# Seven half-block products for the third feed-forward block of a two-layer recurrent trunk

## What is computed

```python
def swiglu(x, wg, wu, wd):
    return (jax.nn.silu(x @ wg) * (x @ wu)) @ wd
...
        x = x + 0.5 * swiglu(rmsnorm(x, ng[0]), prm['ffn_w_gate'][layer, 0], prm['ffn_w_up'][layer, 0], prm['ffn_w_down'][layer, 0])
        hn = rmsnorm(x, ng[1])
...
        x = x + 0.5 * swiglu(rmsnorm(x, ng[2]), prm['ffn_w_gate'][layer, 1], prm['ffn_w_up'][layer, 1], prm['ffn_w_down'][layer, 1])
```

## Time and profile before

| | |
|---|---|
| median of 3 runs | 2454.22 us (2450.13 to 2454.34) |
| the profiled execution | 2454.07 us, span 2452.2 us |
| TensorE (PE) busy | 2386.2 us, 97% |
| VectorE (DVE) busy | 1455.3 us, 59% |
| ScalarE (ACT) busy | 855.2 us, 35% |
| GpSimd (POOL) busy | 399.8 us, 16% |

### The profile page before, as it was taken

The page is one execution under the profiler, slowest core; times in us unless marked ns, Lnnn a source line. Parts: engine busy times, 40 slices in busy tenths (PEclk is TensorE's granted clock), DMA queues, the critical chain, the costliest instruction groups (busy, mean ns, idle before and its releaser), DMA issues.

```text
span 2452.2 us, 44056 instructions
## 1 busy us (share of the span) xinstructions
PE 2386.2 (97%) x18653; PEld 2266.3 (92%) x18653; DVE 1455.3 (59%) x1953; ACT 855.2 (35%) x1198; POOL 399.8 (16%) x524
## 2 busy tenths in 40 slices
PE   7999999999999999999999999999999899999999
PEld 7999999999799999999999999988555589999998
DVE  7856955677755443334343436832788766666654
ACT  5533534453432222223222223334444332222222
POOL 0201200132001122000000000001221113444432
PEclk9999999999999999999999999999999999999999
DMA  4333334232124555332323332322445546888974
GB/s 130 104 104 88 101 89 140 83 87 72 48 78 147 166 157 111 95 88 86 93 87 94 102 91 78 94 71 58 155 155 155 169 134 222 288 296 292 300 240 166
DMA packets 445201, 325.53 MB, mean 133 GB/s; under 512 B 15321, under 2 KB 392453, under 8 KB 444909
## 3 DMA queue, kind: packets, MB, share of 16 engines
q1 hardware_dynamic: 428120, 274.90, 38.2%
q0 software_dynamic: 13232, 42.10, 4.8%
q10 hardware_dynamic: 3728, 6.87, 0.8%
HBM read 278.95 MB, written 44.99 MB: 132 GB/s over the span
## 4 chain that ended last, share of the span: by engine, by line
PE 85%; DVE 8%; DMA 2%; issue 2%; ACT 2%; SPq 0%; POOL 0%; DVEq 0%; POOLq 0%; ACTq 0%
PE ps L2436 65%; PE ps L2529 8%; PE ps L3012 3%; DMA m_c_ring<-in_state_mlstm_C 2%; PE ps L2798 2%; DVE m_qcs L2200 1%; PE ps L2632 1%; PE ps L2940 1%; DVE m_acc L2200 1%; PE ps L2986 0%; PE ps L2927 0%; DVE m_rstd L1494 0%; PE ps L2691 0%; DVE m_tmp L2212 0%; PE ps L2926 0%
## 5 line engine op out<-in xcount | busy, mean ns | idle before, releaser
L2436 PE MATMUL ps<-m_n_hi,m_w_hi 128*128 128x260 f32 x3136 | 635.6, 284 | 5.3 <-DVE m_w_lo L1479 5.3
L2436 PE MATMUL ps<-m_n_hi,m_w_lo 128*128 128x260 f32 x3136 | 632.4, 283 | 0.0
L2436 PE MATMUL ps<-m_n_lo,m_w_hi 128*128 128x260 f32 x3136 | 631.3, 283 | 0.0
L1479 DVE TENSOR_TENSOR m_w_lo<-m_w_raw,m_w_hi 128x1024 fp32r<-128x1024 f32 (+1 forms) x268 | 355.0, 1324 | 327.4 <-ACT m_w_hi L813 276.2
L2436 PEld LDWEIGHTS ps<-m_n_hi,m_w_hi 128*128 128x128 f32 x3136 | 484.3, 189 | 8.5 <-issue 5.0
L2436 PEld LDWEIGHTS ps<-m_n_hi,m_w_lo 128*128 128x128 f32 x3136 | 484.0, 189 | 0.0
L2436 PEld LDWEIGHTS ps<-m_n_lo,m_w_hi 128*128 128x128 f32 x3136 | 482.9, 188 | 0.0
L813 ACT ACTIVATE m_w_hi<-m_w_raw 128x1024 fp32r<-128x1024 f32 (+1 forms) x252 | 279.7, 1110 | 201.0 <-PE ps L2436 194.9
L2436 PE MATMUL ps<-m_h_hi,m_w_hi 128*128 128x260 f32 x1056 | 212.9, 283 | 0.0
L2436 PE MATMUL ps<-m_h_hi,m_w_lo 128*128 128x260 f32 x1056 | 212.3, 282 | 0.0
L2436 PE MATMUL ps<-m_h_lo,m_w_hi 128*128 128x260 f32 x1056 | 211.9, 282 | 0.0
(11 more groups left out here) (518 smaller groups left out, 4082.8 us busy)
## 6 DMA issues: line engine op xcount, KB each, us to landing
m_w_raw<-in_ffn_w_down SPq DMA_DIRECT2D x64, 704.0 KB, 4.7
m_w_raw<-in_ffn_w_gate SPq DMA_DIRECT2D x68, 512.0 KB, 4.2
m_w_raw<-in_ffn_w_up SPq DMA_DIRECT2D x68, 512.0 KB, 4.0
m_c_ring<-in_state_mlstm_C SPq DMA_DIRECT2D x128, 256.0 KB, 3.6
m_u_ring<-in_state_mlstm_C SPq DMA_DIRECT2D x128, 256.0 KB, 5.9
out_C_s<-m_u_ring POOLq DMA_DIRECT2D x128, 256.0 KB, 5.6
m_w_raw<-in_ev_w_in SPq DMA_DIRECT2D x32, 512.0 KB, 4.1
m_w_raw<-in_ml_w_in SPq DMA_DIRECT2D x32, 512.0 KB, 4.1
```

The source lines that it names most:

```text
L1479: v.tensor_tensor(w_lo[:, j % 2, 0:kt * P], w_raw[:, j % 2, 0:kt * P], w_hi[:, j % 2, 0:kt * P].bitcast(F32), ALU.subtract).then_inc(S("w_ ...
L2436: last = mm(out[:, t, :], w[:, j % 2, c], r[:, k0 + k, t * HT:(t + 1) * HT], start=start and k == 0 and n == 0, stop=stop and k == kt - 1 ...
```

## The change

The third FFN takes the seven-product form too: one plain tile (two units) and then 21 blocks, 10 in the first lot and 11 in the second, each lot followed by its 8 down units. The second FFN stays plain, but is done in two lots as well: 22 units, 8 down units that are added to `x`, 22 units, 8 down units. During the last 8 of them the tokens are put in the layout of the third FFN (`n_high_s`, `token_parts`, `token_sums`, `token_high`, `token_low`). The 28 loads of POOL are issued behind the last block of the third FFN, and the transposes and `gate_weights` that use them move into its last 8 down units. In the first FFN, the operations of ACT and DVE around its three plain tiles stand in another order, and the second lot's down units use two pairs of PSUM banks instead of four. Loops of the second and third FFN are written out. The code's helpers have an index `q` now: 0 for the first FFN, 1 for the third.

```diff
--- before.py
+++ after.py
-NP = 3
+STG = (0, 2)
+NPS = (3, 1)
...
+        late_at = (s_at, cur[0] - 4 * T * 4)
...
-        BLOCKS = [(0, i, f) for i, f in enumerate(range(NP, FB))] + [(1, i, f) for i, f in enumerate(range(FB, KF))]
-        FIRST, LAST = (0, FB - NP), (FB - NP - 1, KF - NP - 1)
+        BLOCKS = [(q, c, i, f) for q in range(2) for c in range(2) for i, f in enumerate(range(c * FB if c else NPS[q], (c + 1) * FB))]
...
-        dn_pair = lambda c, d: ((2 + d) % 4, d % 4)[c]
+        dn_pair = lambda c, d: ((2 + d) % 4, d % 2)[c]
...
+                elif c == 0 and i == 0:
+                    sp.wait_ge(S("w_lo"), PLAIN_END[q])
+                elif c == 0 and i == 1:
+                    sp.wait_ge(S("f_tl"), NT * (q + 1))
...
             for i in range(4):
                 pool.wait_ge(S(f"u_kept{i}"), 64)
+            for b in range(FIRST[1][0], len(BLOCKS)):
+                weight_sums(b)
+            pool.wait_ge(S("f_mm"), product(LAST[1][1], "P4"))
...
+            def first_tiles():
+
+                token_high(0, 0)
                 norm_root(0, by_rstd)
                 first_high(4)
-                token_high(1)
                 first_high(5)
-                token_parts(4)
-                token_parts(5)
-                gate(0, 0)
-                token_parts(6)
-                token_parts(7)
-                token_high(2)
-                h_high(0, 0)
-                gate(1, 1)
-                token_high(3)
-                h_high(1, 1)
+                token_high(0, 1)
+                token_parts(0, 4)
+                token_parts(0, 5)
+                gate(0)
+                token_parts(0, 6)
+                token_parts(0, 7)
+                token_high(0, 2)
+                h_high(0)
+                token_high(0, 3)
+                gate(1)
                 a_high(0)
-                gate(2, 2)
+                b_high(0)
+                h_high(1)
+                gate(2)
...
+            def third_tiles():
+
+                token_high(1, 3)
+                a_high(FIRST[1][0])
+                norm_root(NORM_S[1], by_rstd)
+                b_high(FIRST[1][0])
...
+                        if b not in (FIRST[0][0], FIRST[1][0]):
+                            b_high(b)
...
+            def ffn_plain():
+
+                for c in range(2):
+                    u0 = first_unit["up1"] + c * (2 * FB + KD)
+                    for f in range(FB):
+                        u, n = u0 + 2 * f, KF + c * FB + f
+                        hi(u + 1, 1, KD)
+                        if n == KF:
+                            norm_root(NORM_OF[1], by_rstd)
+                            hi(u + 2, 0, KD)
+                        gate(n)
+                        if n > KF:
+                            hi(u + 2, 0, KD if f + 1 < FB else FB)
+                        h_high(n)
+                    u = u0 + 2 * FB
+                    for d in range(KD):
+                        hi(u + d + 1, d + 1, FB if d + 1 < KD else KD)
                         if c:
-                            if d + 2 < KD:
-                                dn_high(c, d + 2)
-                            elif d + 1 == KD:
-                                hi(first_unit["in_e"], 0, KD)
-                            n_high(X_STAGE["dn0"], d)
-                            square(X_STAGE["dn0"], d, d % 2)
-                        else:
-                            if d + 2 < KD:
-                                dn_high(c, d + 2)
-                            if d == 2:
-                                a_high(FIRST[1])
+                            if d + 1 == KD:
+                                hi(u + KD + 1, 1, KD)
+                            n_high_s(1, d)
+                            square(NORM_S[1], d, d % 2)
+                            token_parts(1, d)
+                            if d in (2, 4, 6):
+                                token_high(1, d // 2 - 1)
...
+            def first_tiles():
+
+                token_sums(0, 0)
+                token_sums(0, 1)
+                token_low(0, 0)
                 first_low(4)
-                norm(0, by_rstd)
-                dve.wait_ge(S("r_ev"), 1)
-                plain(0)
                 first_low(5)
-                token_low(1)
-                token_sums(2)
-                plain_up(0)
-                token_low(2)
-                token_sums(3)
-                plain(1)
-                token_low(3)
-                plain_up(1)
+                rows_factor(0)
+                plain(0, 0)
+                token_low(0, 1)
+                token_sums(0, 2)
+                plain_up(0, 0)
+                token_low(0, 2)
+                token_sums(0, 3)
+                token_low(0, 3)
+                plain(1, 2)
+                lot_low(0, A_LOT)
+                plain_up(1, 2)
                 dve.wait_ge(S("f_tl"), NT)
-                h_low(0, 0)
-                h_low(1, 1)
-                lot_low(0, A_LOT)
-                plain(2)
-                plain_up(2)
+                h_low(0)
+                lot_low(0, B_LOT)
+                h_low(1)
+                weight_sums(0)
+                plain(2, 4)
+                plain_up(2, 4)
+
+            def third_tiles():
+
+                b, u = FIRST[1][0], first_unit["up2"]
+                token_sums(1, 3)
+                token_low(1, 3)
+                lot_low(b, A_LOT)
+                lot_low(b, B_LOT)
+                weight_sums(b)
+                rows_factor(NORM_S[1])
+                plain(F0[1], u)
+                lot_low(b, C_LOT)
+                lot_low(b + 1, A_LOT)
+                plain_up(F0[1], u)
...
+                        if q and c and 4 <= d < 7:
+                            gate_weights(d - 4, 0)
+                            gate_weights(d - 4, 1)
+                        down_out(c, d, u, X_R[q] + KD * c, xs)
...
+                    for f in range(FB):
+                        u, n = u0 + 2 * f, KF + c * FB + f
+                        lo(u + 1, 1, KD)
+                        if n == KF:
+                            lo(u + 2, 0, KD)
+                            rows_factor(NORM_OF[1])
+                        plain(n, u)
+                        new_state(u)
+                        if n > KF:
+                            lo(u + 2, 0, KD if f + 1 < FB else FB)
+                        plain_up(n, u)
+                        h_low(n)
+                    if c:
+                        acc_clear(xs)
+                    for d in range(KD):
+                        u = u0 + 2 * FB + d
+                        lo(u + 1, d + 1, FB if d + 1 < KD else KD)
+                        down_out(c, d, u, 2 * KD + KD * c, xs)
+                        if c:
+                            if d + 1 == KD:
+                                lo(u + 2, 1, KD)
+                            n_low_s(1, d)
+                            acc_add(xs, d, d % 2)
+                            if d in (2, 4, 6):
+                                token_low(1, d // 2 - 1)
+                            if d in (1, 3, 5):
+                                token_sums(1, d // 2)
...
+                        if d >= 4 - 2 * c:
+                            pe.wait_ge(S("x_r"), X_R[q] + KD * c + d - 3 + 2 * c)
...
+                        if q and c and d == 4:
+                            pe.wait_ge(S("ld_conv"), 16)
+                            for k in range(KM):
+                                last = nc.tensor.transpose(ps[:, 5, k * NS * 3:(k + 1) * NS * 3], c_stage[:, k * P:(k + 1) * P], ident[0:NS * 3, 0:NS * 3])
+                            last.then_inc(S("cbuf_tr"), 1)
...
-            up(1, 2)
-            down("dn1", KU, 2, h_hi, h_lo, "h_lo", KF)
-            up(2, 3)
-            pe.wait_ge(S("ld_conv"), 16)
-            pe.wait_ge(S("g_r"), 3 * KF)
-            for k in range(KM):
-                last = nc.tensor.transpose(ps[:, 5, k * NS * 3:(k + 1) * NS * 3], c_stage[:, k * P:(k + 1) * P], ident[0:NS * 3, 0:NS * 3])
-            last.then_inc(S("cbuf_tr"), 1)
-            down("dn2", KU, 2, h_hi, h_lo, "h_lo", 2 * KF)
+            ffn_plain()
+            third_tiles()
+            ffn_s(1)
```

More of the change, by code:

```diff
@@ L571, in _ @@
+            ffn_s(0)
             for u, (g, h) in enumerate(EV):
@@ new lines, in third_tiles @@
+            def third_tiles():
+                u0 = first_unit["up2"]
+                for u in range(2):
+                    pe.wait_ge(S("w_lo"), u0 + u + 1)
+                    for k in range(KD):
+                        if u == 0:
+                            pe.wait_ge(S("xn"), KD * NORM_S[1] + k + 1)
+                        last = plain(u, k)
+                    last.then_inc(S("w_mm"), 1)
+                    if u == 0:
+                        norm_sums(NORM_S[1])
+            ffn_s(0)
```

513 lines of the change are left out of this document (288 added, 225 removed).

## The result

The changed kernel takes 2440.05 us, median of 5 runs (2437.97 to 2440.85); the kernel before took 2454.34 beside it (2450.13 to 2458.06). The ratio is 0.9935, 95% interval 0.9923 to 0.9947: 16 us less, between 13 and 19. The profiled execution took 2437.97 us, 16.1 less than before's. Forecast was 2435.9, range 2428 to 2443.

A forecast was written before the change was run, and what follows sets the result against it. TensorE, busy 97% of the span, was taken to bound the kernel. Terms 26.3 - 6.1 - 0.8 - 1.0 - 0.7 + 0.5 = 18.2 us, off 2454.07, gave 2435.9 us, range 2428 to 2443.

The forecast's parts named there:

- The matmuls: In the third FFN 21 tiles change from 11.54 to 10.29 us: 26.3 us less.
- The start: Third FFN's first blocks: PE waits for lots A and C, second lot A and `up_second`: 6.1 us, bounds 0 and 12.
- the clock: Matmuls at TensorE's lower 1.2 GHz level at the third FFN's start: 0.8 us, between 0 and 1.6.
- The second lot: Third FFN's second lot starts like the first FFN's: 0.6 us for lot A, some 0.4 for a copy, 1.0 us.
- The second FFN in two lots: DVE's eight added read-outs and ACT's token work in the last eight units stay hidden: 0 us, bound 3 us.
- The late loads: POOL's 28 loads under the third FFN's last down units hidden; `gate_weights` costs the next stage 0.7 us (0 to 2).
- the rule: GpSimd can't write DMA descriptors while VectorE holds the shared port in a 2-port mode; term taken as 0.
- The first FFN's order: New order around the first FFN's plain tiles: 0.5 us gained, between a loss of 1.5 and 6.8 us.
- Clean starts: Rival, chance 0.07: PE doesn't wait in the first blocks of the third and first FFN; 32.1 us gained, 2422.
- The raw loads: Rival, chance 0.05: third FFN's raw loads take 12 us, every block waits 1.7 us, 2472; decides from 11.2 us.
- DVE's later close: Rival, chance 0.04: DVE's low parts meet POOL twice per block, closing 0.9 us later; P4 waits, no change, 2454.
- The late small loads: Rival, chance 0.04: POOL issues only between DVE's work in down units, so loads land late: 6.5 us, 2442.4.

The follow-up runs named there:

- e1: Changed kernel with DVE's `up_second` ahead of the two weight sums in every block of both FFNs; 2430.71 us, ratio to the kernel before 0.99.
- e2: Changed kernel with ACT's root and DVE's reciprocal ahead of lot A at the third FFN's start; third FFN 362.04 us against 364.50.
- e4: Changed kernel with `gate_weights` one down unit earlier in the third FFN's last eight; third FFN 363.57 us against 364.50.
- e3: Kernel before with only the first FFN's new order of ACT and DVE; 2458.69 us, first FFN 360.96 us against 360.07.
- e5: Changed kernel with 15 blocks' raw loads in the third FFN issued some 6.5 us later; third FFN 365.82 us against 364.50.
- e7: Changed kernel with another order of ACT and DVE around the first FFN's plain tiles; first FFN 355.15 us against 360.66.
- e6: Changed kernel with 15 blocks' raw loads in the third FFN issued some 10.8 us later; third FFN 423.16 us against 364.50.

## Why the prediction was right, and where not

**The matmuls, right.** 84 matmuls in 10.29 us, read in the first FFN's second lot, is what they take in the third FFN. The third FFN as a stage, with the next stage's first unit, became 18.18 us shorter; the forecast's terms for it were 26.3 - 6.1 - 0.8 - 1.0 - 0.7 = 17.7. With what was measured for each (below) they are 26.3 - 6.4 - 0 - 0.7 - 0.7 = 18.5; 0.3 us are left over. PE's busy time was to fall by some 25 us: it fell by 24.0 in the third FFN and by 19.9 in all, as the second mixer has 3.2 us more in this execution and the first FFN 0.9.

**Why a block takes 10.29 us.** I named a chain PE, ACT, DVE, PE with almost no slack. e1 shows the link: DVE does `up_second` only behind the sums. It gave back 1.5 of the 2.0 us that 864 matmuls take above 0.1202 us each.

**The start, right in DVE's queue, wrong in two terms.** I had `up_second` done 28.8 us after the second FFN's last read-out, and it was done at 28.7 us: the long queue of DVE with the reciprocal in it was laid out rightly. From lot A's first product to the fourth product 84 matmuls took 16.5 us, 6.4 more than at 0.1202 us each. The forecast had 6.1 for the waits and 0.8 for the clock, 6.9.

The waits inside came out otherwise: forecast 0.9 us for lot A, 2.3 for lot C, 0.2 for the second lot A and 2.65 for `up_second`; measured 0, 1.77, 0 and 0.86, and 1.61 for lot B. One step that failed is "I take 2.69: 13.3. PE waits 0.9", with "low part of B at 14.9, as PE wants it": who comes second pays, and that was POOL. e2 takes the reciprocal away from between lots B and C, and both waits go.

The other is "I take half, 0.8 us" for the clock. The lower clock came, for 1.6 us, but ahead of a product that had to wait for DVE anyway; e4, with the clock at 1.00, is no faster there (13.36 against 13.34 us). The term belongs at 0. It made the third FFN's sum too small by 0.8 us, while the term for the first FFN, below, was too good by 1.1 us: errors of opposite sign, so it is in part luck that the whole sum is so near.

**The second lot.** Forecast 1.0 us, measured 0.7 for lot A; the 0.4 for a copy is not in the list of waits.

**The second FFN in two lots, right.** 0.00 us (381.43 in both), though ACT was to fit by 0.3 us only.

**The late loads, right.** Nothing for the loads, and 0.70 us at the start of the next stage for `gate_weights`, as worked out; e4 shows that it is this. The rule that the prediction sets against the loads speaks of VectorE in a 2-port mode. No run here shows that DVE's operations beside the loads, tensor-tensor ones for the most part, are in such a mode, so the rule is neither borne out nor refuted by this case.

**The first FFN's order, wrong.** "I take 0.5 us of gain" was a loss of some 0.8 us: 360.66 to 361.14 us in e3 and the five others, against one execution of before, 360.07; it lies within the bound of -1.5. "P1 comes at some 60.8 us" failed: the first product waited 4.0 us for the plain tile's read-out and came 28.1 us after the norm sums, where before has 27.7. And the sum looked at P1 and P6 only. What decides is `up_second`: behind the later read-out of the third plain tile lot C begins 1.8 us later, and the first block's fourth product comes 0.6 us later than before. The lower clock has no part in it (e3 and e5). The bound above, 6.8 us, was real: e7 takes 5.5 of it.

**The rivals.** Clean starts did not come by themselves. The raw loads take some 6 us and were in time. Their border at 10.3 + 0.9 = 11.2 us was put too near; at 12.5 e5 loses 0.1 us per block. Once it is passed, e6 shows 3.9 us per block, with ACT's queue as the carrier. DVE's later close did not come: in a steady block one low part of 1024 columns meets POOL (2.21 us where it takes 1.22 alone) and not two, and the rhythm stays, in e5 within 0.1 us. The late small loads were not late.

**The total.** 18.2 was forecast. The third FFN's 18.2 and the first FFN's -0.6 make 17.6 in the profiled executions, and the beginning and the later stages took another 1.5 back, inside their scatter. The medians beside each other differ by 14.3 us, the ratio says 13 to 19.

## What to carry to other kernels

Cut the execution at landmarks that every version has and compare stage by stage: unchanged stages give the scatter, here larger than most single edits. In a rhythm that many blocks repeat, look at the distance from one matmul to the next and not only at the list of waits; a step that costs 0.15 us and stands wrong once per block is worth more than a wait of 4 us at the start. A stretch at the lower clock is no cost by itself: look at whether the next wait would have held TensorE anyway, and compare an execution that had it with one that had not. And when a transfer is late, ask what stands behind its first reader on that engine: the wait may come out ahead of its user.
